# One layer of a hybrid decoder: residual sums of the last stage on PE, and square roots that take raw sums

## The chip, the cores and the metric

The kernel runs on one core of a Trainium2 chip. The metric is the device time of one execution in microseconds (us). All arithmetic is fp32 but for a few index tables. The engines are PE (matrix products), DVE (vector), ACT (scalar functions), POOL and SP, which here issues most DMAs. The kernel is written engine by engine: each engine runs its own list of instructions in the order written, and the lists meet at semaphores.

## The reference

The whole is one decoder layer on 1024 prompt tokens and 8 x 8 sample tokens, with a convolution group, an RWKV-7 group and a two-level mixture of experts. What matters for the change are the norms:

```python
def rmsnorm(x, g):
    xf = x.astype(jnp.float32)
    y = xf * lax.rsqrt(jnp.mean(xf * xf, axis=-1, keepdims=True) + RMS_EPS)
    return (y * g.astype(jnp.float32)).astype(x.dtype)
...
    xn = rmsnorm(x, norm1_g)
    proj = xn @ w_in
...
    var = jnp.mean(jnp.square(y - mu), axis=-1, keepdims=True)   # per head, in rwkv_mixer
    y_n = ((y - mu) * lax.rsqrt(var + GN_EPS)).reshape(B, T, C_RWKV)
...
    h = x + jnp.concatenate([conv_out, rwkv_out], axis=-1) @ w_out
    h = h + hier_moe(rmsnorm(h, norm2_g), ...)      # each token: the weighted sum of two experts
...
    y_prompt = rmsnorm(h_p, norm_f_g)
    y_sample = rmsnorm(h_s, norm_f_g)
```

D_MODEL is 1024, a head has 64 channels, TOP_K is 2.

## The kernel before

The 1088 tokens are cut into NT = 9 tiles: tiles 0 to 7 have 128 prompt tokens each, tile 8 has the 64 sample tokens. A tile has its tokens on the partitions and 1024 columns.

**Start.** For each tile SP loads the rows of x. ACT squares them with a running total (`square`, L980) and takes the root (`root`, L986); DVE forms mean plus epsilon between the two (`mean_square`, L2151), then the reciprocal and the scaled tile (`scale`, L2157). PE transposes the tile in eight pieces (L1465), and ACT and DVE copy one half of the transposes each (`copy_T`). DVE's loop (L2176 to L2182) is: the mean square of tile i+1, the scaling of tile i, the copy of tile i-1. From tile 5 on PE also does two of the eight steps of the first projection's first piece after each tile (L1472). When all tiles are through, PE transposes the small tables (L1447 to L1454) and goes on with the projection (L1616). The loads are issued in the order: tile 0, the gain, tiles 1 to 8 with two weight loads among them, 18 small tables, further weights.

**Middle.** The group norm of the RWKV part takes its variances with a reduction and then a multiply-add on DVE (`gn_variance`, L2436), a root on ACT (`gn_root`) and a reciprocal on DVE. The second norm has the same chain as the first (`square2` on ACT, `norm2` on DVE), tile by tile, while PE does the output projection.

**Experts.** The turns of the expert loop leave for each token two weighted-to-be rows in DRAM, `y_rows`, and PE, ACT and DVE finish the last group at about the same time.

**Tail.** SP reads the pairs of rows of the nine tiles in the order `LAST`, tile i into `yk[i]` (L734 to L736). `hres[i]`, in SBUF, is the residual of tile i; `w_k` holds the two weights of each token. For the tiles in `ON_PE`, ACT builds two diagonal matrices from the weights (`diag`), and PE forms the weighted sum of the pair in two PSUM banks, `rows_bank(i)`, as products with them: two halves of 512 columns, two rows each (L2134). There are four such pairs of banks, so the fifth and sixth tile wait until DVE has read the first and second (`ff_done`). Ahead of them PE does 72 products of the identity with itself, whose result nobody reads (L2125). On DVE `combine(i)` (L2846) adds the PSUM sum to the residual, or, for the other tiles, does two multiply-adds from `yk` (L2854). ACT squares the result with a running total (L1431), DVE forms mean plus epsilon (`last_mean_square`), ACT takes the root (L1437), and DVE takes the reciprocal and scales by the last gain into `fin[i]` (`last_scale`, L2868). SP stores each tile (L732). DVE's list is a pipeline over three tiles: combine n, mean square n-1, scale n-2.

```python
LAST = [0, NT - 1, 1, 2, 3, 4, *range(5, NT - 1)]
ON_PE = [1, 2, 3, 5, 6, 7]
```

Of the kernel before, what the change touches and what calls it, by code (L numbers as in the profile page):

```python
# [10 lines left out]
ALU = mybir.AluOpType  # L11
# [60 lines left out]
def hybrid_decoder_step(nc, x_prompt, x_sample, state_conv, state_shift, state_wkv, norm1_g, w_in, conv_w, conv_b,  # L72
# [5 lines left out]
    with ctx:  # L78
# [291 lines left out]
        sq_done, ms_done, std_done, xn_done = sem("sq_done"), sem("ms_done"), sem("std_done"), sem("xn_done")  # L370
# [120 lines left out]
        LAST = [0, NT - 1, 1, 2, 3, 4, *range(5, NT - 1)]  # L491
        ON_PE = [1, 2, 3, 5, 6, 7]
# [7 lines left out]
        ff_done, fin_done = sem("ff_done"), sem("fin_done")  # L500
        fin_out = [sem(f"fin_out{s}") for s in range(2)]
# [17 lines left out]
        def _(sp):  # L519
# [213 lines left out]

            for i in LAST:  # L734
                r = rows_of(i)
                sp.dma_start(yk[i][0:r, :, :], y_pairs[i * P:i * P + r, :, :]).then_inc(yk_in[i], 16)  # L736
# [242 lines left out]
        def _(act):  # L979
# [18 lines left out]
            act.wait_ge(iota_done, 1)  # L998
# [194 lines left out]
            def gn_root(i):  # L1193
                v = gvar[:, 0:4 * chunks_of(i)]
                act.wait_ge(gvar_done, i + 1)
                act.activation(v, v, ACT.Sqrt).then_inc(gstd_done, 1)
# [126 lines left out]
            def square2(i):  # L1323
                r = rows_of(i)
                act.wait_ge(h_done, i + 1)
                act.activation(squares2[0:r, :], hres[i][0:r, :], ACT.Square, accum_out=stat[0:r, 4, i:i + 1])\
                    .then_inc(sq_done, 1)
                act.wait_ge(ms_done, NT + i + 1)
                act.activation(stat[0:r, 6, i:i + 1], stat[0:r, 5, i:i + 1], ACT.Sqrt).then_inc(std_done, 1)
# [96 lines left out]
            for n in range(NT + 1):  # L1426
                if n < NT:
                    i = LAST[n]
                    r = rows_of(i)
                    act.wait_ge(ff_done, n + 1)  # L1430
                    act.activation(fin_sq[i][0:r, :], hres[i][0:r, :], ACT.Square, accum_out=stat[0:r, 0, i:i + 1])\  # L1431
                        .then_inc(sq_done, 1)
                if n >= 1:
                    i = LAST[n - 1]
                    r = rows_of(i)
                    act.wait_ge(ms_done, 2 * NT + n)
                    act.activation(stat[0:r, 2, i:i + 1], stat[0:r, 1, i:i + 1], ACT.Sqrt).then_inc(std_done, 1)  # L1437

        @block.tensor
        def _(pe):  # L1440
# [683 lines left out]
            for n in range(72):  # L2124
                pe.matmul(banks(7)[:, 0:P], ident[:, :], ident[:, :], start=True, stop=True)  # L2125
            for n, i in enumerate(ON_PE):
                b = rows_bank(i)
                pe.wait_ge(diag_ready, 2 + n)
                pe.wait_ge(yk_in[i], yk_0[i] + 16)
                if n >= 4:  # L2130
                    pe.wait_ge(ff_done, LAST.index(ON_PE[n - 4]) + 1)
                for half in range(2):
                    for k in range(TOPK):
                        ins = pe.matmul(banks(b + half), diag[:, k, i, :], yk[i][:, k, half * 512:half * 512 + 512],  # L2134
                                        start=(k == 0), stop=(k == TOPK - 1))
                ins.then_inc(rows_psum, 1)

        @block.vector
        def _(dve):
# [9 lines left out]
            dve.memset(stat[:, 7, 2:3], 0.5)  # L2149
            dve.memset(hx[:, :, 0:HB], 0.0)  # L2150
            def mean_square(i):  # L2151
                r = rows_of(i)
                dve.wait_ge(sq_done, i + 1)
                dve.tensor_scalar(stat[0:r, 1, i:i + 1], stat[0:r, 0, i:i + 1], 1.0 / D, RMS_EPS, ALU.mult, ALU.add)\
                    .then_inc(ms_done, 1)

# [279 lines left out]
            def gn_variance(i):  # L2436
                v = gvar[:, 0:4 * chunks_of(i)]
                dve.wait_ge(gsq_done, i + 1)
                dve.wait_ge(yn_done, i)
                link(dve.tensor_reduce(v, groups(gsq[i], i), AX.X, ALU.add))  # L2440
                dve.tensor_scalar(v, v, 1.0 / HD, GN_EPS, ALU.mult, ALU.add).then_inc(gvar_done, 1)
# [149 lines left out]
            def norm2(i):  # L2591
                r = rows_of(i)
                dve.wait_ge(sq_done, NT + i + 1)
                dve.tensor_scalar(stat[0:r, 5, i:i + 1], stat[0:r, 4, i:i + 1], 1.0 / D, RMS_EPS, ALU.mult, ALU.add)\
                    .then_inc(ms_done, 1)
# [250 lines left out]
            def combine(i):  # L2846
                r = rows_of(i)
                if i in ON_PE:
                    dve.wait_ge(rows_psum, NT + ON_PE.index(i) + 1)
                    dve.tensor_tensor(hres[i], banks(rows_bank(i), 2), hres[i], ALU.add).then_inc(ff_done, 1)  # L2850
                    return
# [9 lines left out]
            def last_mean_square(n):  # L2861
                i = LAST[n]
                r = rows_of(i)
                dve.wait_ge(sq_done, 2 * NT + n + 1)
                dve.tensor_scalar(stat[0:r, 1, i:i + 1], stat[0:r, 0, i:i + 1], 1.0 / D, RMS_EPS, ALU.mult, ALU.add)\
                    .then_inc(ms_done, 1)

            def last_scale(n):  # L2868
# [6 lines left out]
                dve.wait_ge(ff_done, n + 1)  # L2875
                dve.scalar_tensor_tensor(out=fin[i][0:r, :], in0=hres[i][0:r, :], scalar=stat[0:r, 3, i:i + 1],
                                         in1=gain_f[0:r, :], op0=ALU.mult, op1=ALU.mult).then_inc(fin_done, 1)

            for n in range(NT + 2):
                if n < NT:  # L2880
# [36 lines left out]
```

## Time and profile before

| | us |
|---|---|
| median of 3 runs | 1195.33 |
| the runs | 1194.43, 1199.28, 1195.33 |
| the profiled execution, its own time | 1193.24 |
| its span in the profile | 1191.5 |
| PE busy | 1125.2 (94% of the span) |
| DVE busy | 669.5 (56%) |
| ACT busy | 362.9 (30%) |
| mean granted clock of PE, as a share of full speed | 0.977 |

In the chain of work that ended last, the products of the input projection (L1616) have 27%, those of the expert loop (L2077, L2107) 15% and 8%, the output projection (L1927) 9%. Busy times of PE are modelled, so the start of a product is to be trusted more than its length. Times in the rows count from the start of the span.

### The profile page before, as it was taken

Reading aid. Unit: us, or ns where it says so; the run is one execution under the profiler, and the core shown is the slowest. Engines: PE = TensorE matmul, PEld = TensorE weight load, DVE = VectorE, ACT = ScalarE, POOL = GpSimd, SP = SyncE. Lnnn points to the kernel's source line nnn. Section 1 sums busy time; section 2 is a strip of 40 time slices with the busy share of each in tenths; the row PEclk is TensorE's granted clock in tenths of the full one; section 3 lists DMA queues with packets and bytes.
Section 4 is the critical chain, followed back from the end, with each engine's and each line's share of the span. In section 5 each row is a group of like instructions: output and inputs, shape, how many; then the busy total and the mean of one; then the engine's idle time right before and its main releaser. Section 6 shows DMA issues by size and latency. Waiting matters only on the chain.

```text
span 1191.5 us, 24463 instructions
## 1 busy us (share of the span) xinstructions
PE 1125.2 (94%) x9496; PEld 683.2 (57%) x9497; DVE 669.5 (56%) x1177; ACT 362.9 (30%) x722; POOL 221.0 (19%) x280
## 2 busy tenths in 40 slices
PE   5999999999998899999989999986999999999986
PEld 4666666666556688998985555544333333333362
DVE  5188999992224578888853332455434343434327
ACT  5100001111212556767742221122133232322232
POOL 5000000010002212333320011001223333333100
PEclk9999999999999899999999999987999999999999
DMA  9111111110000111111125322138899899999657
GB/s 288 51 36 36 36 37 38 41 42 22 1 1 5 16 16 17 16 20 19 19 48 189 106 62 71 45 138 337 340 372 323 306 331 342 415 411 407 267 180 311
DMA packets 97293, 171.44 MB, mean 144 GB/s; under 512 B 44377, under 2 KB 68624, under 8 KB 87921
## 3 DMA queue, kind: packets, MB, share of 16 engines
q1 hardware_dynamic: 89713, 152.31, 36.1%
q0 software_dynamic: 7488, 17.84, 4.3%
q8 instruction: 66, 1.08, 0.4%
q14 instruction: 26, 0.21, 0.1%
HBM read 153.63 MB, written 25.91 MB: 151 GB/s over the span
## 4 chain that ended last, share of the span: by engine, by line
PE 84%; DVE 9%; DMA 2%; ACT 2%; issue 2%; SPq 0%; DVEq 0%; ACTq 0%; POOLq 0%
PE ps L1616 27%; PE ps L2077 15%; PE ps L1927 9%; PE ps L2107 8%; PE ps L1628 6%; PE ps L1649 3%; PE ps L2064 2%; DVE arena L2390 1%; PE ps L1637 1%; PE ps L2125 1%; PE ps L1957 1%; DVE arena L2393 1%; PE ps L1515 1%; DMA arena<-in_w_exp_up_dram 1%; PE ps L2134 1%
## 5 line engine op out<-in xcount | busy, mean ns | idle before, releaser
L1616 PE MATMUL ps<-arena 128*128 128x384 f32 (+1 forms) x1040 | 318.9, 468 | 0.0
L1616 PEld LDWEIGHTS ps<-arena 128*128 128x128 f32 x1040 | 196.9, 190 | 118.6 <-issue 1.4
L2077 PE MATMUL ps<-arena 128*64 x416 | 188.5, 596 | 3.1 <-DVE arena L2791 2.2
L2080 PE MATMUL ps<-arena 128*64 128x512 f32 x416 | 188.5, 596 | 0.0
L2227 DVE SCALAR_TENSOR_TENSOR arena<-arena,cw 128x1024 f32<-128x1024 f32 x240 | 168.2, 778 | 0.4
L2077 PEld LDWEIGHTS ps<-arena 128*64 128x64 f32 x416 | 54.5, 136 | 111.3 <-issue 111.3
L1927 PE MATMUL ps<-arena 128*128 128x512 f32 x256 | 113.1, 596 | 0.0
L1628 PE MATMUL ps<-arena 64*64 64x64 f32 x2960 | 100.0, 219 | 6.6 <-DMA arena<-x_blocks 1.9
L1628 PEld LDWEIGHTS ps<-arena 64*64 64x64 f32 x2960 | 93.1, 135 | 10.0 <-issue 5.4
L2107 PE MATMUL ps<-arena 128*64 x208 | 96.5, 607 | 2.4 <-ACT arena L1395 2.4
L2110 PE MATMUL ps<-arena 128*64 128x512 f32 x208 | 96.5, 607 | 0.0
L1927 PEld LDWEIGHTS ps<-arena 128*128 128x128 f32 x256 | 47.5, 190 | 57.1 <-issue 57.0
L839 POOL COPY lastz<-arena 128x1 f32<-128x1 f32 x14 | 11.4, 813 | 328.8 <-ACT arena L1113 328.8
L1107 ACT ACTIVATE arena<-ps 128x768 f32<-128x768 f32 x14 | 11.4, 812 | 195.8 <-PE ps L1616 195.8
L933 POOL DMA_INDIRECT late<-xn_rows,g_idx x24 | 64.5, 2686 | 20.4 <-POOL g_idx L930 20.4
L2812 DVE COPY arena<-arena 128x4096 f32 x26 | 59.4, 2283 | 8.2 <-SPq L674 6.4
L2797 DVE TENSOR_TENSOR small<-ps,small 128x256 f32<-128x256 f32 x26 | 11.0, 425 | 89.7 <-ACT small L1379 89.7
L2280 DVE TENSOR_TENSOR arena<-arena 128x1024 f32<-128x1024 f32 x14 | 17.1, 1222 | 72.0 <-ACT arena L1113 72.0
L2107 PEld LDWEIGHTS ps<-arena 128*64 128x64 f32 x208 | 26.8, 138 | 53.0 <-issue 53.0
L2080 PEld LDWEIGHTS ps<-arena 128*64 128x64 f32 x416 | 54.5, 136 | 0.0
L2821 DVE COPY arena<-ps 128x256 f32<-128x256 f32 x26 | 11.0, 424 | 76.6 <-PE ps L2093 76.6
L1395 ACT ACTIVATE arena<-arena 128x2048 f32 x26 | 49.6, 1908 | 14.1 <-SPq L678 12.9
(357 smaller groups left out, 1552.4 us busy)
## 6 DMA issues: line engine op xcount, KB each, us to landing
arena<-in_w_exp_gate_dram SPq DMA_DIRECT2D x32, 1024.0 KB, 8.2
arena<-in_w_exp_up_dram SPq DMA_DIRECT2D x32, 1024.0 KB, 10.9
arena<-in_w_exp_down_dram SPq DMA_DIRECT2D x32, 1024.0 KB, 10.0
arena<-in_w_in_dram SPq DMA_DIRECT2D x22, 512.0 KB, 4.1
arena<-in_x_prompt_dram SPq DMA_DIRECT2D x16, 512.0 KB, 7.8
arena<-y_rows SPq DMA_DIRECT2D x8, 1024.0 KB, 15.1
arena<-in_w_out_dram SPq DMA_DIRECT2D x2, 2048.0 KB, 10.6
xn_rows<-arena SPq DMA_DIRECT2D x8, 512.0 KB, 2.9
```

The source lines that it names most:

```text
L933: pool.indirect_dma_start(out=xg[b], out_offset=None, in_=xn2_rows, in_offset=bass.IndirectOffsetOnAxis(ap=g_idx[b][:, :], axis=0), bounds ...
L1395: act.activation(wd.rearrange("p c n -> p (c n)"), wring[:, bass.ds(slot, 1), 2 * DC * F:].rearrange("p a n -> p (a n)"), ACT.Copy)\
L1616: ins = pe.matmul(banks(proj_bank(q) + piece)[:, 0:n1 - n0], win[q % 6][:, c, :], xnT[:, c, n0:n1], start=(c == 0), stop=(c == DC - 1))
L1628: ins = pe.matmul(dst[h, hp * 64:hp * 64 + 64], lhs[h, hp, :], rhs[h, hp, :], start=alone or (first and hp == 0), stop=alone or last, skip ...
L1649: ins = pe.matmul(banks(2 + c)[h, hp * P:(hp + 1) * P], lhs[h, hp, t], AR[j % 3][h, hp, :, t], start=True, stop=True)
L1927: ins = pe.matmul(banks(2 * (i % 2) + half)[0:r, :], lhs, wout[c // CT][:, c % CT, half * 512:half * 512 + 512], start=(c == 0), stop=(c = ...
L2077: pe.matmul(banks(b)[0:HS, :], xgT[b][:, c, 0:HS], wring_gu[:, bass.ds(slot, 1), 0:2, c, :].rearrange("p a w f -> p (a w) f"), start=(c == ...
L2080: ins = pe.matmul(banks(b)[HS:P, :], xgT[b][:, c, HS:P], wgu[b][:, :, c, :], start=(c == 0), stop=(c == DC - 1))
L2107: pe.matmul(banks(5 + half)[0:HS, :], hT[:, c, 0:HS], wring[:, bass.ds(slot, 1), n0:n0 + 512].rearrange("p a n -> p (a n)"), start=(c == 0 ...
L2110: ins = pe.matmul(banks(5 + half)[HS:P, :], hT[:, c, HS:P], wd[:, c, half * 512:half * 512 + 512], start=(c == 0), stop=(c == 1))
L2227: dve.scalar_tensor_tensor(out=dst, in0=src, scalar=w, in1=dst, op0=ALU.mult, op1=ALU.add).then_inc(conv_tap, 1)
L2812: dve.tensor_copy(wgu[b].rearrange("p w c f -> p (w c f)"), wring[:, bass.ds(slot, 1), 0:2 * DC * F].rearrange("p a n -> p (a n)"))\
```

## The change

There are four parts.

1. Two constants, RMS_EPS and GN_EPS, are written to `stat` once, and each root takes the raw sum, with 1/D or 1/HD as its scale and the constant as its bias. The mean squares on DVE are gone, in all three norms and in the group norm. ACT waits for its own square instead.
2. In the tail five tiles (1, 2, 3, 5, 6) are on PE, and tile 7 joins 0, 4 and 8 on DVE. PE also adds the residual, as a product with the identity that opens each sum in PSUM; for the first four tiles ahead of all row pairs. The unread products ahead are 48 instead of 72. The fifth tile waits for the scaling of the first (`fin_done`).
3. ACT's square and DVE's last scaling read the complete sum of such a tile straight from PSUM. `combine` is left for tiles 0, 8, 4 and 7 alone.
4. DVE's list in the tail is written out anew, and the order of tiles 6 and 7 is exchanged in the scalings and the stores. The rows are read in the same order as before (`READ`).

```diff
-        LAST = [0, NT - 1, 1, 2, 3, 4, *range(5, NT - 1)]
-        ON_PE = [1, 2, 3, 5, 6, 7]
+        LAST = [0, NT - 1, 1, 2, 3, 4, 5, 7, 6]
+        ON_PE = [1, 2, 3, 5, 6]
...
+        def summed(i):
+            return banks(rows_bank(i), 2) if i in ON_PE else hres[i][0:rows_of(i), :]
...
             def root(i):
                 r = rows_of(i)
-                act.wait_ge(ms_done, i + 1)
-                act.activation(stat[0:r, 2, i:i + 1], stat[0:r, 1, i:i + 1], ACT.Sqrt).then_inc(std_done, 1)
+                act.wait_ge(sq_done, i + 1)
+                act.activation(stat[0:r, 2, i:i + 1], stat[0:r, 0, i:i + 1], ACT.Sqrt, scale=1.0 / D,
+                               bias=rms_eps[0:r, :]).then_inc(std_done, 1)
...
-            for n in range(72):
+            for n in range(48):
                 pe.matmul(banks(7)[:, 0:P], ident[:, :], ident[:, :], start=True, stop=True)
+
+            def residual_in(i):
+                for half in range(2):
+                    pe.matmul(banks(rows_bank(i) + half), ident[:, :], hres[i][:, half * 512:half * 512 + 512],
+                              start=True, stop=False)
+
+            for i in ON_PE[0:4]:
+                residual_in(i)
             for n, i in enumerate(ON_PE):
                 b = rows_bank(i)
                 pe.wait_ge(diag_ready, 2 + n)
+                if n == 4:
+                    pe.wait_ge(fin_done, LAST.index(ON_PE[0]) + 1)
+                    residual_in(i)
                 pe.wait_ge(yk_in[i], yk_0[i] + 16)
-                if n >= 4:
-                    pe.wait_ge(ff_done, LAST.index(ON_PE[n - 4]) + 1)
...
-            mean_square(0)
             for i in range(NT):
-                if i + 1 < NT:
-                    mean_square(i + 1)
                 scale(i)
                 if i >= 1:
                     copy_T(i - 1)
...
-                dve.wait_ge(ff_done, n + 1)
-                dve.scalar_tensor_tensor(out=fin[i][0:r, :], in0=hres[i][0:r, :], scalar=stat[0:r, 3, i:i + 1],
+                dve.scalar_tensor_tensor(out=fin[i][0:r, :], in0=summed(i), scalar=stat[0:r, 3, i:i + 1],
                                          in1=gain_f[0:r, :], op0=ALU.mult, op1=ALU.mult).then_inc(fin_done, 1)
 
-            for n in range(NT + 2):
-                if n < NT:
-                    combine(LAST[n])
-                if 1 <= n <= NT:
-                    last_mean_square(n - 1)
-                if n >= 2:
-                    last_scale(n - 2)
+            combine(LAST[0])
+            combine(LAST[1])
+            for n in range(NT):
+                last_scale(n)
+                if n == 3:
+                    combine(4)
+                if n == 6:
+                    combine(7)
```

DVE's list at the start of the program, before. `arena<-arena,stat,gain` is the scaling, `arena<-ps` the copy of transposes:

```order
L2154 TENSOR_SCALAR stat<-stat 128x1 [waits sq_done] x2
L2160 RECIPROCAL stat<-stat 128x1 [waits std_done]
L2165 SCALAR_TENSOR_TENSOR arena<-arena,stat,gain 128x1024 [waits gain1_in,dve_chain]
L2154 TENSOR_SCALAR stat<-stat 128x1 [waits sq_done]
L2160 RECIPROCAL stat<-stat 128x1 [waits std_done]
L2165 SCALAR_TENSOR_TENSOR arena<-arena,stat,gain 128x1024 [waits dve_chain]
L2172 COPY arena<-ps 128x4x128 [waits xT_psum]
```

The same place in the changed kernel:

```order
L2174 RECIPROCAL stat<-stat 128x1 [waits std_done]
L2179 SCALAR_TENSOR_TENSOR arena<-arena,stat,gain 128x1024 [waits gain1_in,dve_chain]
L2174 RECIPROCAL stat<-stat 128x1 [waits std_done]
L2179 SCALAR_TENSOR_TENSOR arena<-arena,stat,gain 128x1024 [waits dve_chain]
L2186 COPY arena<-ps 128x4x128 [waits xT_psum]
```

The scaling of tile 0 no longer has an instruction ahead of it that waits for tile 1's square.

DVE's list in the tail, before, from tile 8's multiply-adds on to the scaling of tile 1 (`shift` is the buffer of `w_k`, `late` the last gain):

```order
L2854 SCALAR_TENSOR_TENSOR arena<-arena,shift 64x1024 [waits dve_chain]
L2865 TENSOR_SCALAR stat<-stat 128x1 [waits sq_done]
L2850 TENSOR_TENSOR arena<-ps,arena 128x1024 [waits gb_psum]
L2865 TENSOR_SCALAR stat<-stat 64x1 [waits sq_done]
L2872 RECIPROCAL stat<-stat 128x1 [waits std_done]
L2876 SCALAR_TENSOR_TENSOR arena<-arena,stat,late 128x1024 [waits ff_done,tables2_in,dve_chain]
L2850 TENSOR_TENSOR arena<-ps,arena 128x1024 [waits gb_psum]
L2865 TENSOR_SCALAR stat<-stat 128x1 [waits sq_done]
L2872 RECIPROCAL stat<-stat 64x1 [waits std_done]
L2876 SCALAR_TENSOR_TENSOR arena<-arena,stat,late 64x1024 [waits ff_done,dve_chain]
```

The changed kernel, from the scaling of tile 2 to that of tile 5:

```order
L2871 SCALAR_TENSOR_TENSOR arena<-ps,stat,late 128x1024 [waits dve_chain]
L2857 SCALAR_TENSOR_TENSOR arena<-arena,shift 128x1024 [waits w_loaded4]
L2857 SCALAR_TENSOR_TENSOR arena<-arena,shift 128x1024 [waits dve_chain]
L2868 RECIPROCAL stat<-stat 128x1 [waits std_done]
L2871 SCALAR_TENSOR_TENSOR arena<-ps,stat,late 128x1024 [waits dve_chain]
L2868 RECIPROCAL stat<-stat 128x1 [waits std_done]
L2871 SCALAR_TENSOR_TENSOR arena<-arena,stat,late 128x1024 [waits dve_chain]
L2868 RECIPROCAL stat<-stat 128x1 [waits std_done]
L2871 SCALAR_TENSOR_TENSOR arena<-ps,stat,late 128x1024 [waits dve_chain]
```

The additions and mean squares are out of the list, the scalings of tiles on PE read `ps`, and tile 4's multiply-adds stand between the scalings of tiles 2 and 3.

PE's list in the tail of the changed kernel (before, the 72 unread products were followed by six groups of four row-pair products and nothing else):

```order
L2134 MATMUL ps<-ident 128x128 x47
L2138 MATMUL ps<-arena,ident 128x512 x8
L2152 MATMUL ps<-arena 128x512 [waits w_loaded1,tanh_done]
L2152 MATMUL ps<-arena 128x512 x3
L2152 MATMUL ps<-arena 128x512 [waits w_loaded2,tanh_done]
L2152 MATMUL ps<-arena 128x512 x3
L2152 MATMUL ps<-arena 128x512 [waits w_loaded3,tanh_done]
...
L2138 MATMUL ps<-arena,ident 128x512 [waits fin_done,tanh_done]
L2138 MATMUL ps<-arena,ident 128x512
L2152 MATMUL ps<-arena 128x512 [waits x_loaded0]
```

Eight residual products (`arena,ident`) now stand between the unread products and tile 1's row pairs, and two more ahead of tile 6's.

## Rows read from the trace of the kernel before

**Rows 1.** The page's chain that ended last, shares of the span by engine.

```profile
PE 84%; DVE 9%; DMA 2%; ACT 2%; issue 2%; SPq 0%; DVEq 0%; ACTq 0%; POOLq 0%
```

**Rows 2.** Timeline of SP: start, length, engine, line, operation, out<-in, count.

```profile
1.26 0.42 SPq L530 DMA_DIRECT2D gain<-in_norm_g_dram  x1
...
8.90 4.89 SPq L522 DMA_DIRECT2D arena<-in_x_sample_dram  x1
...
21.56 7.79 SPq L526 DMA_DIRECT2D arena<-in_w_in_dram  x4
```

**Rows 3.** The same loads in the DMA view: count, KB, us from issue to landing.

```profile
gain<-in_norm_g_dram SPq DMA_DIRECT2D x1, 512.0 KB, 5.2
...
arena<-in_x_sample_dram SPq DMA_DIRECT2D x1, 256.0 KB, 12.6
...
arena<-in_w_in_dram SPq DMA_DIRECT2D x1, 512.0 KB, 8.1
```

**Rows 4.** Timeline of DVE at the start; in brackets the idle time before.

```profile
9.21 1.28 DVE L2165 SCALAR_TENSOR_TENSOR arena<-arena,stat,gain 128x1024 f32<-128x1024 f32 x1
...
21.81 0.15 DVE L2160 RECIPROCAL stat<-stat 128x1 f32<-128x1 f32 x1
...
23.20 0.69 DVE L2172 COPY arena<-ps 128x512 f32<-128x512 f32 x1
```

**Rows 5.** PE at the start: timeline, then stretches of L1465 (after the dash PEclk, DMA, GB/s).

```profile
23.34 1.97 PE L1465 MATMUL ps<-ident,arena 128*128 128x128 f32 x8 [0.95 <-DVE arena L2165]
...
33.54 0.26 PE L1447 MATMUL ps<-ident,arena 50*128 50x50 f32 x1
...
15.90:19.80 3.90, 3.77 (x16) 3.13 (x16) 1.00 1.08 255
21.30:22.40 1.10, 1.09 (x8) 0.85 (x8) 1.00 1.06 232
23.30:25.30 2.00, 1.96 (x8) 1.57 (x8) 0.50 1.04 225
```

**Rows 6.** Timeline of ACT at the start, the root of tile 1.

```profile
9.14 0.20 ACT L989 ACTIVATE stat<-stat 128x1 f32<-128x1 f32 x1 [0.22 <-DVE stat L2154]
```

**Rows 7.** Timeline of ACT near 518 us, without and with a bias from SBUF.

```profile
518.06 0.63 ACT L1024 ACTIVATE arena<-arena 128x512 f32<-128x512 f32 x1 [0.41 <-DVE arena L2235]
518.72 0.72 ACT L1026 ACTIVATE arena<-arena,stat 128x512 f32<-128x512 f32 x1
```

**Rows 8.** The chain in order of time, second norm of tile 8: start, length, what.

```profile
790.89 0.16 DVE stat L2594
```

**Rows 9.** Timeline of DVE in the tail.

```profile
1154.30 2.60 DVE L2854 SCALAR_TENSOR_TENSOR arena<-arena,shift 128x1024 f32<-128x1024 f32 x2 [9.90 <-DMA arena<-y_rows]
...
1164.33 1.22 DVE L2850 TENSOR_TENSOR arena<-ps,arena 128x1024 f32<-128x1024 f32 x1 [4.57 <-PE ps L2134]
...
1171.20 1.22 DVE L2850 TENSOR_TENSOR arena<-ps,arena 128x1024 f32<-128x1024 f32 x1 [0.77 <-PE ps L2134]
...
1187.16 1.29 DVE L2876 SCALAR_TENSOR_TENSOR arena<-arena,stat,late 128x1024 f32<-128x1024 f32 x1
```

**Rows 10.** Groups by line and shape, 1143 to 1192: count, busy us, mean ns, idle before.

```profile
L2850 DVE TENSOR_TENSOR arena<-ps,arena 128x1024 f32<-128x1024 f32 x6 | 7.3, 1221 | 6.1 <-PE ps L2134 6.1
...
L1431 ACT ACTIVATE arena<-arena 128x1024 f32<-128x1024 f32 x8 | 8.5, 1057 | 23.4 <-DVE arena L2850 13.0 <-DVE arena L2854 10.4
...
L1431 ACT ACTIVATION_READ_ACCUMULATOR arena<-arena 128x1 f32 x8 | 1.5, 187 | 0.0
```

**Rows 11.** Lines 2125 and 2134 on PE: ns min/median/max, first and last start.

```profile
L2125 PE MATMUL ps<-ident x144: 275/275/347, 1144.5 to 1160.6; 128*128 128x128 f32 x144
...
L2134 PE MATMUL ps<-arena x48: 592/592/595, 1160.7 to 1180.9; 128*128 128x512 f32 x48
```

**Rows 12.** Line 736, the nine reads of row pairs: ns each, first and last issue.

```profile
L736 SPq DMA_DIRECT2D arena<-y_rows x9: 344/469/655, 1148.6 to 1152.9; - x9
...
DMA to landing us min/median/max: 5.7/15.1/21.8
```

More of the change, by code:

```diff
@@ L490, in hybrid_decoder_step @@
         diag = at(O_ZS + NT * D, TOPK, NT, P)
-        LAST = [0, NT - 1, 1, 2, 3, 4, *range(5, NT - 1)]
-        ON_PE = [1, 2, 3, 5, 6, 7]
+        READ = [0, NT - 1, *range(1, NT - 1)]
+        LAST = [0, NT - 1, 1, 2, 3, 4, 5, 7, 6]
+        ON_PE = [1, 2, 3, 5, 6]
+        ON_DVE = [i for i in LAST if i not in ON_PE]
+        assert len(ON_PE) == 5 and len(LAST) == NT
         diag_ready, rows_psum = tanh_done, gb_psum
@@ L732, in result_out @@
                 sp.dma_start(dst, fin[i][0:r, :]).then_inc(fin_out[n % 2], 16)
-            for i in LAST:
+            for i in READ:
                 r = rows_of(i)
@@ L1195, in gn_root @@
                 act.wait_ge(gvar_done, i + 1)
-                act.activation(v, v, ACT.Sqrt).then_inc(gstd_done, 1)
+                act.activation(v, v, ACT.Sqrt, scale=1.0 / HD, bias=gn_eps).then_inc(gstd_done, 1)
             def gn_affine(i, b):
@@ L1327, in square2 @@
                     .then_inc(sq_done, 1)
-                act.wait_ge(ms_done, NT + i + 1)
-                act.activation(stat[0:r, 6, i:i + 1], stat[0:r, 5, i:i + 1], ACT.Sqrt).then_inc(std_done, 1)
+                act.wait_ge(sq_done, NT + i + 1)
+                act.activation(stat[0:r, 6, i:i + 1], stat[0:r, 4, i:i + 1], ACT.Sqrt, scale=1.0 / D,
+                               bias=rms_eps[0:r, :]).then_inc(std_done, 1)
             def copy_T2(i):
@@ L1425, in _ @@
             act.activation(stat[:, 7, 0:1], stat[:, 7, 1:2], ACT.Sqrt)
-            for n in range(NT + 1):
-                if n < NT:
[L1428 to L1437, printed above, removed]
+            for n in range(NT):
+                i = LAST[n]
+                r = rows_of(i)
+                if i in ON_PE:
+                    act.wait_ge(rows_psum, NT + ON_PE.index(i) + 1)
+                else:
+                    act.wait_ge(ff_done, ON_DVE.index(i) + 1)
+                act.activation(fin_sq[i][0:r, :], summed(i), ACT.Square, accum_out=stat[0:r, 0, i:i + 1])\
+                    .then_inc(sq_done, 1)
+                act.wait_ge(sq_done, 2 * NT + n + 1)
+                act.activation(stat[0:r, 2, i:i + 1], stat[0:r, 0, i:i + 1], ACT.Sqrt, scale=1.0 / D,
+                               bias=rms_eps[0:r, :]).then_inc(std_done, 1)
         @block.tensor
@@ L2134, in _ @@
                         ins = pe.matmul(banks(b + half), diag[:, k, i, :], yk[i][:, k, half * 512:half * 512 + 512],
-                                        start=(k == 0), stop=(k == TOPK - 1))
+                                        start=False, stop=(k == TOPK - 1))
                 ins.then_inc(rows_psum, 1)
@@ L2149, in _ @@
             dve.memset(stat[:, 7, 2:3], 0.5)
+            dve.memset(stat[:, 7, 4:5], RMS_EPS)
+            dve.memset(stat[:, 7, 5:6], GN_EPS).then_inc(eps_ready, 1)
             dve.memset(hx[:, :, 0:HB], 0.0)
[L2151 to L2155, printed above, removed]
             def scale(i):
@@ L2439, in gn_variance @@
                 dve.wait_ge(yn_done, i)
-                link(dve.tensor_reduce(v, groups(gsq[i], i), AX.X, ALU.add))
-                dve.tensor_scalar(v, v, 1.0 / HD, GN_EPS, ALU.mult, ALU.add).then_inc(gvar_done, 1)
+                dve.tensor_reduce(v, groups(gsq[i], i), AX.X, ALU.add).then_inc(gvar_done, 1)
             def gn_inverse(i):
@@ L2859, in combine @@
                 ins.then_inc(ff_done, 1)
[L2861 to L2866, printed above, removed]
             def last_scale(n):
@@ L2874, in last_scale @@
                     dve.wait_ge(tables2_in, 16 * 6)
[L2875 to L2876 removed]
+                dve.scalar_tensor_tensor(out=fin[i][0:r, :], in0=summed(i), scalar=stat[0:r, 3, i:i + 1],
                                          in1=gain_f[0:r, :], op0=ALU.mult, op1=ALU.mult).then_inc(fin_done, 1)
[L2879 to L2885 removed]
+            combine(LAST[0])
+            combine(LAST[1])
+            for n in range(NT):
+                last_scale(n)
[3 more added lines that the diff above has]
+                    combine(7)
 _INS = ['x_prompt', 'x_sample', 'state_conv', 'state_shift', 'state_wkv', 'norm1_g', 'w_in', 'conv_w', 'conv_b',
```

12 lines of the change are left out of this document (3 added, 9 removed).

## Prediction

> **What bounds the kernel now.** I read the page's chain first [rows 1]: PE carries 84% of it and DVE 9%, so an operation removed from DVE or ACT gains time only in the stretches where the chain leaves PE. I then went through the chain in order of time for each place that the diff touches. There are four: the start (tile norms ahead of the first projection), the group norm and the second norm (mostly beside PE's work), and the tail. In the start and in the tail DVE and ACT set the pace, and there I read each engine's own timeline.
>
> The profiled execution took 1193.24 us with a span of 1191.5. The shown runs have a median of 1195.33, so the sum below is made against 1193.24 and then carried over to the median. A difference of 0.5% is 6 us, about what a measurement of this kernel can tell from none.
>
> **Start: DVE's order loses a wait.** Before, DVE did the mean square of tile i+1 ahead of the scaling of tile i. Its scaling of tile 0 thus stood behind tile 1's square sum: it began at 9.21 us [rows 4], though tile 0's root had long been taken. With the mean squares gone, tile 0's scaling waits for its root and for the gain alone. The gain's load is issued at 1.26 and lands 5.2 us later [rows 2, 3], at about 6.5. That is 2.7 us earlier for the first transposes, and ACT, which copies tile 0's transposes before it squares tile 3, moves up as well.
>
> After that each tile needs on DVE a reciprocal, a scaling and a copy. From reciprocal to the end of the copy these take 21.81 to about 23.85 [rows 4], so 2.05 us. Before, the scalings of tiles 0 and 5 began at 9.21 and 22.0 (right behind the reciprocal at 21.81) [rows 4], 2.55 us a tile, because DVE's extra wait for the next tile's sum closed a ring DVE, PE, ACT, DVE over two tiles. Afterwards I place tile 1's scaling at 9.4 (its square waits for its data and its root ended at 9.34 [rows 6], now near 9.2) and then one tile in 2.05 us: tile 5's scaling starts at 9.4 + 4 x 2.05 = 17.6 and ends at 18.8. Before, PE began tile 5's transposes at 23.34 [rows 5], and from there it was busy up to 33.54, where the transposes of the tables begin: 10.2 us for four tiles and the interleaved eight-column pieces of the first projection. Same work from 18.8 ends at 29.0, that is 4.5 us earlier. PE goes on with the projection at once, and DVE, ACT and the later weight loads follow PE by their waits, so I see nothing that gives this back.
>
> Both ends of this term: the pace of PE's transposes differs by two within the start (16 passes in 3.8 us between 15.9 and 19.8, 8 in 1.1 us between 21.3 and 22.4, 8 in 2.0 us from 23.3 on; the clock is printed as 1.00 for the first two and 0.50 for the third [rows 5]). If PE is quick from tile 5 on, its four tiles need about 8.5 us, and the end is 27.3; but there the data stops it. Tile 8's rows land at 8.90 + 12.6 = 21.5, which still fits. The tables are issued before the weights that are issued at 21.56 and land 8.1 us later, at 29.7 [rows 2, 3]; that load is 0.5 MB, so the tables are there some 2 us sooner, near 27.9. This makes the largest gain 5.6 us. If the transposes of all four tiles run slowly, as 23.3 shows, they take 3 x 1.1 us more than in the quick case, and the end is about 30.5, a gain of 3. If the tables land just with the weights at 29.7, the gain is 3.8. I take 4.5, since rows 5 show one slow tile in this stretch and I leave it in.
>
> **The roots themselves.** ACT's root of a tile now takes the raw sum, with a bias read from SBUF, and waits for ACT's own square. Removed: ACT's idle time of 0.22 us ahead of a root [rows 6], less a few hundredths for the new wait. Added: the bias operand. No root with one is in the trace; the nearest pair is ACT's 0.722 us with such a bias against 0.630 without, same shape [rows 7], so 0.09. Net 0.1 us a tile for the better. In the start it is inside the 9.4 above. In the second norm and the group norm PE works on meanwhile. The chain meets such a step at tile 8 of the second norm, 0.16 us at 790.89 [rows 8], and once in the group norm, about as long. Sum for both, less the bias: **0.3 us**, with ends 0 and 0.5.
>
> **Tail: the DVE list.** Before, DVE's last stretch ran from the row pairs of tile 0 at 1154.30 to the end of the last scaling at 1188.45, and from 1171.20 on it hardly idled [rows 9]. Its work there: 3 tiles of two multiply-adds, 6 additions of PE's pair sum to the residual (1.22 us each [rows 10]), 9 mean squares, 9 reciprocals and 9 scalings. The change takes away the 6 additions and the mean squares (7.3 us and about 0.06 of its own time for each mean square, 0.5) and puts in one more tile of multiply-adds, 2.55 us: DVE loses 5.3 us of work. It doesn't get all of it, since now every scaling waits in turn for its square and root, with nothing of another tile between.
>
> PE first. The 144 passes of the 72 dummy products last from 1144.5 to 1160.6 [rows 11], 0.112 us each; 96 passes end at 1155.3. Then come the residuals of four tiles, two products of 512 columns a tile. A product is two passes in the trace (24 products of row pairs gave 48 passes between 1160.7 and 1180.9, 0.43 us each [rows 11]), so these are 16 passes, 6.9 us. The first pair sum thus starts at 1162.2, not at 1160.7; the rows are there, since the nine reads land 5.7 to 21.8 us after their issues from 1148.6 to 1152.9 [rows 12], the last one (tile 7) at 1174.7. With 8 passes a tile, 3.43 us, and 0.2 until DVE sees the sum (1164.33 in [rows 9] for 1160.7), the sums of tiles 1, 2, 3 and 5 are ready at 1165.8, 1169.2, 1172.6 and 1176.0, and tile 6, with its own residual (12 passes), at 1181.2. Its wait for the third scaling costs nothing: that is done near 1168.6.
>
> From a sum to its scaling: a square of 1.06 and a read of its total of 0.19, which overlap by 0.1 [rows 10]; a root of 0.20 [rows 6] and 0.09 for its bias, and DVE's reciprocal, 0.19 before the scaling can start. That is about 1.4 + 0.2; a scaling takes 1.2 in a row of them. Walking down DVE's list:
> - tile 2's scaling starts at 1170.85 and ends at 1172.1 (DVE idles ahead of it);
> - tile 4's multiply-adds end at 1174.6, tile 3's scaling at 1176.0;
> - tile 4's at 1177.5 (ACT just keeps up), tile 5's at 1179.0;
> - tile 7's multiply-adds end at 1181.5; DVE waits 1.5 us for its square and root, and scales it by 1184.4;
> - tile 6's, ready on PE at 1181.2, is squared after tile 7's and scaled by 1185.9.
>
> Against 1188.45 this is **2.5 us** earlier. The same walk with the old list gives 1188.4, so its durations fit. The stores behind it stay: 3 us from the last scaling to the end of the span, as before.
>
> What bounds this term: no scaling from PSUM is in the trace. DVE's addition from PSUM takes 1.22 us [rows 10] and a scaling from SBUF 1.29 [rows 9], so PSUM need cost nothing; with 0.13 more for each of them and 0.1 more for ACT's squares the walk ends at 1186.6 (gain 1.8), with 0.05 less each and a root as short as before at 1185.4 (gain 3.0). The Trainium skill (VectorE: DVE Perf Modes, the section on the TRN2 errata) gives DVE 58 cycles of fixed cost from SBUF and 120 from PSUM, at 0.96 GHz an estimate of 0.06 us more for each of the scalings from PSUM; by it the tail's gain would be 2.3 instead of 2.5. The rows on the 1024-wide operations speak against it here.
>
> **Sum.** 4.5 + 0.3 + 2.5 = 7.3 us. On the profiled execution that gives 1185.9, on the median of the shown runs 1188.0. Profiled and plain runs can fall either side, so I forecast 1187.5.
>
> **Rivals.**
> *Start holds, tail doesn't (chance 0.12).* If PE's sums come a few us late (they are on the path up to tile 2, and again if tile 6's sum passes 1182.8), DVE waits and the tail ends where it did. For it: before, DVE had idled 4.6 us for tile 1 [rows 9], and the residuals delay that sum by another 1.5. Against: DVE has 5.3 us less to do. Time: 1195.3 - 4.8 = 1190.5.
> *Tail holds, start doesn't (0.17).* The ring in the start is really held by the data, or the pace of transposes halves, or the tables land late. For it: DMA moves data all through the first 30 us, and the tables come last. Against: the landings above. Left are 0.3 + 2.5 and perhaps 0.5: 1192.
> *Slower (0.05).* PE's clock falls in the tail. The dummy products are what keeps PE busy while the rows travel; a third of them goes. At the low level, where a transpose took 0.25 us instead of 0.14 or less [rows 5], each pass of 512 columns would take twice 0.43, 0.86. The path to tile 2's sum has 32 of them: 13.7 us more, less the 7.3, so 6.4 above the median: 1201.7. It decides from 17 slow passes on. Against: PE goes from dummies to residuals to pair sums with no idle time from 1144.5 to 1181.
> *The change does nothing* would be that DVE's wait for the root replaces the wait for the sum everywhere; that is true of the second norm and is counted there.
>
> **How the numbers follow.** My forecast has the rest, 0.66. Its own range follows from the bounds: gains of 3.0 to 5.6, 0 to 0.5, 1.8 to 3.0, so 4.8 to 9.1 below 1193.2 or 1195.3: 1184 to 1190.5. Taking in the second rival up to 1192.5 leaves out some 0.15. Over 0.5% faster means below 1189.4: 0.52 of my 0.66 (7.3 is not far above 6, and three runs spread by a few us), 0.04 of the first rival, 0.01 of the second: 0.57. Slower: 0.05 and a noisy pair of medians, 0.06. The rest, 0.37, is the same.
>
> **What would show it.** In the start: tile 0's scaling near 6.5, DVE at one tile in 2.05 us, the table transposes near 29. If they start at 31 or later, that step is wrong. In the tail: dummies up to 1155.3 (counted from their start, 10.8 us), first pair sum 17.7 us after it; DVE idle ahead of tiles 1, 2 and 7's scalings only; last scaling 31.6 us after the first multiply-add, where it was 34.15. Roots of 0.28 us. In between: the same distance from the table transposes to the first row read, within 1 us; if that distance grows, the gain of the start was given back there.

## The result and the profile after

The changed kernel takes 1186.70 us (median of 12 runs, 1182.63 to 1191.58) against 1194.47 for the kernel before (12 runs of the same comparison, 1191.49 to 1199.28). The ratio is 0.9936 with a 95% interval of 0.9922 to 0.9951: faster by 7.6 us, give or take 1.7. The forecast was 1187.5, from a sum of 7.3 us.

The profiled execution took 1186.2 us with a span of 1184.5, 7.0 us less than before. The stages, by their first instructions in the two traces, in us:

| stretch | before | after | difference |
|---|---|---|---|
| start of the span to the transposes of the tables | 33.54 | 28.26 | -5.3 |
| from there to the first unread product | 1111.0 | 1111.6 | +0.6 |
| from there to the end of the last scaling | 43.90 | 41.54 | -2.4 |
| from there to the end of the span | 3.05 | 3.10 | 0.0 |

DVE's timeline at the start of the changed kernel (start, length, engine, line, operation, count, in brackets the idle time before and what ended it):

```profile
5.92 0.16 DVE L2174 RECIPROCAL stat<-stat 128x1 f32<-128x1 f32 x1 [4.69 <-ACT stat L996]
6.64 1.28 DVE L2179 SCALAR_TENSOR_TENSOR arena<-arena,stat,gain 128x1024 f32<-128x1024 f32 x1 [0.56 <-DMA gain<-in_norm_g_dram]
9.37 0.17 DVE L2174 RECIPROCAL stat<-stat 128x1 f32<-128x1 f32 x1 [1.44 <-ACT stat L996]
...
18.15 1.28 DVE L2179 SCALAR_TENSOR_TENSOR arena<-arena,stat,gain 128x1024 f32<-128x1024 f32 x1
```

Tile 0's scaling starts at 6.64 instead of 9.21 ([rows 4]), and what it waits for is now the gain's load. The last line is tile 5, which starts at 18.15 where it started at 22.00. PE in the same stretch, from tile 4 on:

```profile
17.50 1.09 PE L1474 MATMUL ps<-ident,arena 128*128 128x128 f32 x8 [1.31 <-DVE arena L2179]
19.49 1.09 PE L1474 MATMUL ps<-ident,arena 128*128 128x128 f32 x8 [0.90 <-DVE arena L2179]
20.42 1.46 PE L1481 MATMUL ps<-arena 128*128 128x384 f32 x4
...
28.26 0.26 PE L1456 MATMUL ps<-ident,arena 50*128 50x50 f32 x1
```

Tile 5's transposes start at 19.49 instead of 23.34 and take 1.09 us, not 1.97 ([rows 5]).

ACT's root of tile 1, which answers to [rows 6], follows the read of the total at once. It is longer, 0.29 us for 0.20, so it ends at 9.33, where it ended at 9.34:

```profile
8.82 0.19 ACT L990 ACTIVATION_READ_ACCUMULATOR arena<-arena 128x1 f32 x1
9.04 0.29 ACT L996 ACTIVATE stat<-stat 128x1 f32<-128x1 f32 x1
```

The tail on DVE, from the scaling of tile 1 on:

```profile
1162.82 1.28 DVE L2871 SCALAR_TENSOR_TENSOR arena<-ps,stat,late 128x1024 f32<-128x1024 f32 x1
1166.06 0.16 DVE L2868 RECIPROCAL stat<-stat 128x1 f32<-128x1 f32 x1 [1.95 <-ACT stat L1445]
1166.26 1.28 DVE L2871 SCALAR_TENSOR_TENSOR arena<-ps,stat,late 128x1024 f32<-128x1024 f32 x1
1167.46 2.59 DVE L2857 SCALAR_TENSOR_TENSOR arena<-arena,shift 128x1024 f32<-128x1024 f32 x2
...
1174.39 2.60 DVE L2857 SCALAR_TENSOR_TENSOR arena<-arena,shift 128x1024 f32<-128x1024 f32 x2
1178.53 0.16 DVE L2868 RECIPROCAL stat<-stat 128x1 f32<-128x1 f32 x1 [1.54 <-ACT stat L1445]
...
1180.12 1.28 DVE L2871 SCALAR_TENSOR_TENSOR arena<-ps,stat,late 128x1024 f32<-128x1024 f32 x1
```

DVE idles 1.95 us ahead of tile 2's reciprocal and 1.54 ahead of tile 7's, and ends at 1181.40. PE's list behind it, without a gap from the unread products to the last row pair:

```profile
1139.86 10.96 PE L2134 MATMUL ps<-ident 128*128 128x128 f32 x96 [0.88 <-DVE small L2836]
1150.65 7.03 PE L2138 MATMUL ps<-arena,ident 128*128 128x512 f32 x16
1157.52 13.90 PE L2152 MATMUL ps<-arena 128*128 128x512 f32 x32
1171.25 1.88 PE L2138 MATMUL ps<-arena,ident 128*128 128x512 f32 x4
```

The operations on PSUM, in groups by line and shape (count, busy us, mean ns, idle before), DVE's scalings and then ACT's squares:

```profile
L2871 DVE SCALAR_TENSOR_TENSOR arena<-ps,stat,late 128x1024 f32<-128x1024 f32 x5 | 6.4, 1284 | 0.2
L2871 DVE SCALAR_TENSOR_TENSOR arena<-arena,stat,late 128x1024 f32<-128x1024 f32 x3 | 3.9, 1285 | 0.1
...
L1442 ACT ACTIVATE arena<-ps 128x1024 f32<-128x1024 f32 x5 | 5.1, 1017 | 8.9 <-PE ps L2152 8.9
L1442 ACT ACTIVATE arena<-arena 128x1024 f32<-128x1024 f32 x3 | 3.2, 1057 | 13.0 <-DVE arena L2857 13.0
```

### The profile page after: what moved, and what is told of

Read it like the earlier page. It is cut to its first block, busy times and chain, and to the rows that moved or that the text cites. A ratio compares the mean times of both kernels' runs of the same rounds, so it can differ in the third digit from the quotient of the medians.

```text
span 1184.5 us, 24342 instructions
## 1 busy us (share of the span) xinstructions
PE 1123.2 (95%) x9460; PEld 679.1 (57%) x9461; DVE 658.5 (56%) x1139; ACT 366.4 (31%) x720; POOL 223.9 (19%) x280
## 3 DMA queue, kind: packets, MB, share of 16 engines
q1 hardware_dynamic: 89713, 152.31, 36.2%
## 4 chain that ended last, share of the span: by engine, by line
PE 82%; DVE 10%; DMA 4%; ACT 2%; issue 2%; SPq 1%; DVEq 0%; ACTq 0%; POOLq 0%
PE ps L1625 27%; PE ps L2086 13%; PE ps L1936 9%; PE ps L2116 7%; PE ps L1637 6%; DMA arena<-in_w_exp_up_dram 3%; PE ps L1658 3%; PE ps L2073 2%; DVE arena L2401 1%; PE ps L1646 1%; PE ps L1966 1%; PE ps L2134 1%; DVE arena L2404 1%; PE ps L1524 1%; DVE arena L2367 1%
## 6 DMA issues: line engine op xcount, KB each, us to landing
arena<-in_w_out_dram SPq DMA_DIRECT2D x2, 2048.0 KB, 10.5
```

## The experiments

Theory: the start gains because DVE's wait for tile i+1's sum no longer stands ahead of tile i's scaling; the tail gains because DVE has less to do, with PE on the path up to tile 2's sum; the middle neither gains nor loses. The rivals: the gain of the start comes from the removed operations and their handovers; a later stage gives it back; the tail is bound by one engine alone.

Eight kernels were run, 4 to 12 times each: four on one chip beside 31 runs of the kernel before, and four on another beside 14. Below, "tables" is the first transpose of the tables, and "tail" is the time from the first unread product on PE to the start of the last scaling on DVE; each is read from the run's profile.

| kernel | ratio to before (95%) | tile 0's scaling | tables | tail |
|---|---|---|---|---|
| before | 1 | 9.2 | 33.5 | 42.6 |
| changed | 0.9936 (0.9922 to 0.9951) | 6.6 | 28.3 | 40.3 |
| start alone | 0.9943 (0.9921 to 0.9965) | 6.7 | 28.5 | 42.7 |
| mean squares kept, moved | 0.9979 (0.9958 to 0.9999) | 6.6 | 30.3 | 42.6 |
| changed, one wait put back | 0.9965 (0.9949 to 0.9981) | 9.3 | 34.2 | 40.3 |
| tail alone | 0.9970 (0.9953 to 0.9986) | 9.3 | 34.2 | 40.3 |
| changed, DVE's list reordered | 0.9914 (0.9896 to 0.9932) | 6.6 | 28.2 | 38.4 |
| the same with 40 unread products | 0.9872 (0.9851 to 0.9893) | 6.7 | 29.1 | 36.6 |
| changed, 72 unread products | 0.9964 (0.9946 to 0.9982) | 6.7 | 28.3 | 45.6 |
| reordered with 24 | 0.9898 (0.9874 to 0.9921) | 6.6 | 28.3 | 36.2 |

The ratio isn't the quotient of the two medians. These alone give 5.8 us less for the start alone, 3.0 with the wait put back and 13.8 for the one with 40, each inside the interval of its ratio but nearer to zero than the ratio says.

**The start alone.** The kernel before with the first norm's part of the change:

```diff
-                act.wait_ge(ms_done, i + 1)
-                act.activation(stat[0:r, 2, i:i + 1], stat[0:r, 1, i:i + 1], ACT.Sqrt).then_inc(std_done, 1)
+                act.wait_ge(sq_done, i + 1)
+                act.activation(stat[0:r, 2, i:i + 1], stat[0:r, 0, i:i + 1], ACT.Sqrt, scale=1.0 / D,
+                               bias=rms_eps[0:r, :]).then_inc(std_done, 1)
...
-            mean_square(0)
             for i in range(NT):
-                if i + 1 < NT:
-                    mean_square(i + 1)
                 scale(i)
```

> The kernel before, with the mean squares taken off DVE in the first norm alone (ACT's root takes the raw sum with a bias there). Theory: the gain of the start stands alone and PE keeps it; table transposes begin at 28.3 us (33.5 before), the whole is 5.3 us shorter, give or take 1.5 for stretches of low PE clock that fall elsewhere. Rival (the later stages give part of it back): table transposes at 28.3, but the whole under 3 us shorter.

Measured: tables at 28.5, and 0.9943, 6.8 us less (4.2 to 9.4). The gain of the start stands alone, and the plain runs keep it whole. The profiled execution alone would not have shown this: its span is 1188.2, only 3.3 less than before, since its middle took 1.7 us more (below). The transposes of the tables waited here for a load that they need, so the last of those loads landed near 28.5 in this run, and a shorter list on DVE can hardly bring the start below that:

```profile
28.54 0.26 PE L1450 MATMUL ps<-ident,arena 50*128 50x50 f32 x1 [0.22 <-DMA late<-in_w_gate_up_dram]
```

**The mean squares kept, but moved.** The kernel before with this edit alone; every operation is still done, and the root still waits for DVE:

```diff
-            mean_square(0)
             for i in range(NT):
-                if i + 1 < NT:
-                    mean_square(i + 1)
+                mean_square(i)
                 scale(i)
```

> The kernel before, with every mean square still on DVE, but in the first norm the one of tile i directly ahead of the scaling of tile i instead of the one of tile i+1. Theory (the place in DVE's list costs, not the operation): scaling of tile 0 near 6.6 us, tiles 2.3 us apart, table transposes near 30.3, about 3.3 us earlier than before. Rival (the operation and its handover through DVE cost): scaling of tile 0 early too, but the table transposes stay at 32.5 or later.

Measured: tile 0's scaling at 6.60, tiles from 1 on 2.4 to 2.7 us apart, tables at 30.3. DVE's timeline, the scalings of tiles 0, 1, 2 and 5:

```profile
6.60 1.28 DVE L2165 SCALAR_TENSOR_TENSOR arena<-arena,stat,gain 128x1024 f32<-128x1024 f32 x1 [0.64 <-DMA gain<-in_norm_g_dram]
...
9.61 1.28 DVE L2165 SCALAR_TENSOR_TENSOR arena<-arena,stat,gain 128x1024 f32<-128x1024 f32 x1
...
12.02 1.32 DVE L2165 SCALAR_TENSOR_TENSOR arena<-arena,stat,gain 128x1024 f32<-128x1024 f32 x1
...
19.38 0.17 DVE L2160 RECIPROCAL stat<-stat 128x1 f32<-128x1 f32 x1 [0.27 <-ACT stat L989]
19.58 1.29 DVE L2165 SCALAR_TENSOR_TENSOR arena<-arena,stat,gain 128x1024 f32<-128x1024 f32 x1
```

So 3.2 of the 5.3 us come with no operation removed, by its place in DVE's list. Of the remaining 2.0, 1.4 are there when tile 5's scaling starts (19.58 for 18.15). In this kernel the sum goes ACT, DVE, ACT, DVE for each tile, and DVE idles 0.27 us ahead of each reciprocal for ACT's root. The other 0.6 lie behind it, where PE's transposes of tile 5 took 1.70 us and not 1.09.

**One wait put back.** The changed kernel with a wait and no operation:

```diff
             for i in range(NT):
+                if i + 1 < NT:
+                    dve.wait_ge(sq_done, i + 2)
                 scale(i)
```

> The changed kernel, with one wait put back and no operation: ahead of the scaling of tile i in the first norm, DVE waits for the square sum of tile i+1. Theory (the wait closes the ring): scaling of tile 0 at 9.1 us again, table transposes at 33, the whole about 5 us longer than the changed kernel, so 2 to 3 us shorter than before. Rival (mean squares and handovers cost): tile 0 late, but the table transposes by 30.5, since tiles then follow at 2.05 us.

Measured: tile 0's scaling at 9.29, tables at 34.20. PE's timeline at tile 5 (the first line) and the tables:

```profile
23.49 1.97 PE L1474 MATMUL ps<-ident,arena 128*128 128x128 f32 x8 [0.88 <-DVE arena L2179]
...
34.20 0.26 PE L1456 MATMUL ps<-ident,arena 50*128 50x50 f32 x1
```

That is where the kernel with the tail alone has them (34.2), whose start is that of the kernel before. With the wait in place, taking nine mean squares off DVE is worth nothing that shows here. I had expected 33; the profiles of two kernels with the same start as before lie 0.7 us apart (33.5 and 34.2), which covers a part of the miss of 1.2. The whole is 4.2 us shorter than before (2.3 to 6.1), where 2 to 3 were expected; that is inside the interval.

**The tail alone.** The changed kernel with the first norm, the group norm and the second norm as before (the edit of the first norm is the reverse of the one above; nothing in the tail differs from the changed kernel). For the second norm:

```diff
-                act.wait_ge(sq_done, NT + i + 1)
-                act.activation(stat[0:r, 6, i:i + 1], stat[0:r, 4, i:i + 1], ACT.Sqrt, scale=1.0 / D,
-                               bias=rms_eps[0:r, :]).then_inc(std_done, 1)
+                act.wait_ge(ms_done, NT + i + 1)
+                act.activation(stat[0:r, 6, i:i + 1], stat[0:r, 5, i:i + 1], ACT.Sqrt).then_inc(std_done, 1)
...
+                dve.wait_ge(sq_done, NT + i + 1)
+                dve.tensor_scalar(stat[0:r, 5, i:i + 1], stat[0:r, 4, i:i + 1], 1.0 / D, RMS_EPS, ALU.mult, ALU.add)\
+                    .then_inc(ms_done, 1)
```

> The kernel before, with the change made in the tail alone; first norm, group norm and second norm as before. Theory: from the first unread product on PE to the end of the last scaling 41.5 us instead of 43.9, the whole 2.4 us shorter, give or take 1.5. Rival (the tail's gain needs the earlier parts, or comes from noise): below 1 us.

Measured: tail 40.3 instead of 42.6, and 3.6 us less in all (1.7 to 5.6). The stages agree with the table of the first section: 5 to 5.3 us from the start, 2.4 from the tail. The 6.8 us of the start alone and the 3.6 here add up to 10.4, more than the 7.6 of the whole change, but the three intervals are wide enough for that. The change to the group norm and the second norm was not run by itself.

**DVE's list reordered.** The changed kernel with the two multiply-add pairs one scaling earlier:

```diff
-                if n == 3:
+                if n == 2:
                     combine(4)
-                if n == 6:
+                if n == 5:
                     combine(7)
```

> The changed kernel, with tile 4's multiply-adds one scaling earlier on DVE (behind tile 1's scaling) and tile 7's one earlier (behind tile 4's). Theory (the tail's end hangs on DVE, which idles 2 us ahead of tile 2's reciprocal and 1.5 ahead of tile 7's): 1.8 us shorter; from the first unread product to the start of the last scaling 38.4 us instead of 40.2, and DVE idles under 0.5 us ahead of tile 7's reciprocal. Rival (PE's sums set the end): tile 6's sum is no earlier, under 0.5 us gained.

Measured: tail 38.4. DVE's timeline:

```profile
1159.65 2.59 DVE L2857 SCALAR_TENSOR_TENSOR arena<-arena,shift 128x1024 f32<-128x1024 f32 x2
1162.16 0.16 DVE L2868 RECIPROCAL stat<-stat 128x1 f32<-128x1 f32 x1
...
1172.05 0.16 DVE L2868 RECIPROCAL stat<-stat 128x1 f32<-128x1 f32 x1 [0.15 <-ACT stat L1445]
```

Tile 4's multiply-adds now fill the time ahead of tile 2's reciprocal, and DVE waits 0.15 us for tile 7's root, not 1.54. So in the changed kernel the end of the tail hung on the order of DVE's list, not on PE's last sum, which comes no earlier here (36.7 us after the first unread product in both). Now it does hang on it: ACT waits 0.21 us for PE's sum of tile 6 before its last square. What is left of DVE's idle time is 1.48 us ahead of tile 3's reciprocal and the wait for tile 1's sum.

**The same with 40 unread products.** The added edit:

```diff
-            for n in range(48):
+            for n in range(40):
```

> As the run before, with 40 unread products instead of 48. Theory (PE is on the path through the sums of tiles 1 and 2, and the rows of tile 1 have landed by then): all sums 1.8 us earlier, and the tail 36.6 us. Rival (the rows land later than thought, or DVE is the only bound): 38 us or more.

Measured: tail 36.6, and a ratio of 0.9872, the lowest of all, though the interval overlaps that of the run with 24. By the plain runs that is 15.3 us less than before (12.8 to 17.8); by the stages it is 4.5 from the start and 6.0 from the tail, so 10.5 (the two spans differ by 10.8). The difference of 5 us isn't accounted for by stages; part of it can be the scatter of the middle, and 1.5 of it goes if the medians are compared.

**72 unread products.** The changed kernel with:

```diff
-            for n in range(48):
+            for n in range(72):
```

> The changed kernel with the 72 unread products of before instead of 48. Theory (PE on the path up to tile 2's sum): every sum 5.4 us later, the tail 45.6 us instead of 40.2, so 3 us longer than that of the kernel before. Rival (DVE alone sets the end): the tail grows by under 2 us.

Measured: tail 45.6, 5.4 us more than with 48. That is 48 passes by 0.112 us, all of it on the path. PE's timeline and DVE's wait for tile 1:

```profile
1141.94 16.32 PE L2134 MATMUL ps<-ident 128*128 128x128 f32 x144 [0.89 <-DVE small L2836]
1158.10 7.03 PE L2138 MATMUL ps<-arena,ident 128*128 128x512 f32 x16
...
1170.07 0.16 DVE L2868 RECIPROCAL stat<-stat 128x1 f32<-128x1 f32 x1 [10.79 <-ACT stat L1445]
```

With the residuals on PE and the unread products as many as before, the tail is thus 3 us longer than that of the kernel before (45.6 for 42.6). The cut from 72 to 48 is not a trimming beside the change but what makes the tail's part pay. The opposite test, the kernel before with fewer unread products, was not run, and it is a rival for the tail. In that kernel DVE idled 4.57 us for tile 1's sum [rows 9]. Its first row pair could start some 1.7 us earlier before it met the landing of tile 1's rows (14.5 us after the first unread product in the last run below, where it started at 16.15). So an estimated 1.7 of the tail's 2.4 us might have come from fewer unread products alone; the 6.0 us of the reordered list with 40 are beyond that estimate.

**24 unread products, reordered.** The kernel with the reordered list and:

```diff
-            for n in range(48):
+            for n in range(24):
```

> As the run with 40, with 24 unread products. PE then has residual products up to 1150 us or so and idles about 5 us until tile 1's rows land. If PE keeps its clock over that idle time: tail 36.6 us, as with 40, since the rows set the start. If the clock falls to the low level in it: passes of 512 columns take 0.86 us for some us, and the tail is 39 us or more.

Measured: tail 36.2. PE idled 2.0 us for tile 1's rows, and its passes kept their length, at a granted clock of 1.00 throughout. DVE waited for rows too, the last of them tile 7's:

```profile
1142.63 7.03 PE L2138 MATMUL ps<-arena,ident 128*128 128x512 f32 x16
1151.67 13.97 PE L2152 MATMUL ps<-arena 128*128 128x512 f32 x32 [2.01 <-DMA arena<-y_rows]
```

```profile
1167.63 2.61 DVE L2857 SCALAR_TENSOR_TENSOR arena<-arena,shift 128x1024 f32<-128x1024 f32 x2 [1.03 <-DMA arena<-y_rows]
```

The idle time was 2.0 us and not the 5 I had written (the residual products alone last 6.9), so this doesn't show what a longer one does. It does show that fewer unread products help only until the rows bound the tail: tile 1's land near 1151.7 - 1137.2 = 14.5 us after the first one, and tile 7's near 30.4. The last scaling starts 0.5 us earlier than with 40, but what follows it up to the end of the span takes 3.85 us and not 3.21, so from the first unread product to the end it is 41.3 us against 41.1. Going from 40 to 24 gains nothing.

## Why the prediction was right

**The start.** Both halves of the argument hold: the scaling of tile 0 waits for the gain (6.64, predicted 6.5), tile 1's starts at 9.57 (9.4), and tile 5's at 18.15 (17.6). The moved mean squares and the wait put back show that the cause is the wait in DVE's order. The term came out as 5.3 us where 4.5 was taken, inside its 3.0 to 5.6, from two errors of opposite sign. Tile 5's transposes began at 19.49 and not at 18.8, since tile 4's scaling took 1.73 us instead of 1.28 and tile 1's root ended no earlier than before. From there to the tables PE took 8.8 us and not 10.2: I had left one slow tile in that stretch, as [rows 5] had it, and its pace was mis-sized. In the changed kernel the transposes ran slowly for tiles 0 to 2 alone and quickly from 15.05 on. (The interleaved work that I called eight-column pieces is products of 384 columns.) The tables' landing, which I had put near 27.9, didn't hold PE at 28.26, so it was no later than that; with the start alone it held PE until 28.54. My upper bound of 5.6 was thus nearly reached.

**Nothing gives it back.** Shown in the plain runs by the start alone (6.8 us less, 4.2 to 9.4) and, less directly, by the changed kernel.

**The middle.** Predicted 0.3 us less, measured 0.6 more in the pair of profiles. The local step did shrink: at tile 8 of the second norm ACT gets from its square to the end of the root in 1.47 us, where it took 1.63:

```profile
784.72 1.06 ACT L1334 ACTIVATE arena<-arena 64x1024 f32<-64x1024 f32 x1 [7.76 <-DVE arena L2597]
785.68 0.19 ACT L1334 ACTIVATION_READ_ACCUMULATOR arena<-arena 64x1 f32 x1
785.90 0.29 ACT L1337 ACTIVATE stat<-stat 64x1 f32<-64x1 f32 x1
```

But the middle as a whole scatters far more than that: from the tables to the first unread product the profiles show 1109.2 to 1112.7 us for the four kernels with the middle of before, and 1107.3 to 1113.6 for the six with the changed one. In one stretch the cause is plain. From the last product of line 1589 of the kernel before to the first of line 1927, the six kernels with the changed middle (changed, 72, wait put back, 40, reordered, 24) took 79.2, 79.2, 77.9, 77.2, 76.6 and 76.5 us. The first two have a granted clock below 1 in two places of it, the next two in one, the last two in none. The changed kernel, two stretches of 4 us (busy us and instructions of PE, PEld, DVE, ACT, POOL, then PEclk, DMA share, GB/s):

```profile
592.00:596.00 4.00, 4.00 (x92) 4.00 (x89) 3.58 (x8) 0.77 (x2) 0.95 (x1) 0.57 0.71 159
620.00:624.00 4.00, 4.00 (x100) 4.00 (x99) 2.28 (x5) 3.22 (x7) 0.00 (x0) 0.66 0.97 334
```

and the reordered one:

```profile
592.00:596.00 4.00, 4.00 (x130) 4.00 (x128) 2.28 (x4) 3.02 (x10) 1.04 (x1) 1.00 0.63 140
620.00:624.00 4.00, 2.74 (x94) 2.60 (x90) 1.84 (x3) 0.97 (x3) 1.04 (x1) 1.00 1.02 414
```

PE is busy throughout in both at 592, with 92 matrix instructions in 4 us at the low clock and 130 at the full one. The 0.3 us were never measurable in the whole.

**Luck in the sum.** The three terms came to 7.0 us against 7.3 because their errors cancel: the start gave 0.8 more than taken, the middle 0.9 less, which is scatter, and the tail 0.1 less. The terms of the start and the tail are borne out by themselves; the closeness of the sum is not a merit of theirs.

**The tail.** Step by step against the first unread product at 1139.86: predicted first residual 10.8 us after it, measured 10.79; tile 1's sum 21.25, ACT starts on it at 21.29; tile 2's scaling 26.3, measured 26.40; end of tile 7's multiply-adds 36.95, measured 37.1; end of the last scaling 41.35, measured 41.54. The term was 2.4 for 2.5. That PE is on the path up to tile 2's sum is shown by the run with 72. The reordered list shows that the two idle times of DVE which the walk found were the ones that counted. What the walk doesn't say is how much of the 2.4 us the smaller number of unread products would have brought by itself (see the run with 72).

**PSUM as a source.** DVE's scaling takes 1.284 us from PSUM and 1.285 from SBUF, and ACT's square 1.017 from PSUM and 1.057 from SBUF. By the Trainium skill's table (VectorE: DVE Perf Modes, the section on the TRN2 errata) the scaling should have been about 0.06 us longer from PSUM, an estimate. The trace shows no difference; for ACT the table's 52 cycles less from PSUM, at its 1.2 GHz an estimate of 0.043 us, agree with the 0.040 measured.

**The rivals.** None came about. The slower one, a fall of PE's clock in the tail, has nothing for it: the passes keep their 0.43 us even with a third of the original unread products and an idle time of 2 us. From what stretch of idleness they would slow down was not tried.

## What to carry to other kernels

In an in-order engine, look at what a cheap operation waits for, not at what it costs: a 0.15 us operation for the next tile, put ahead of the work on this one, tied DVE, PE and ACT into a ring by its wait, and cost 5 us in nine tiles. Moving it alone brought three of them, and removing it with the wait left in place brought none. When work is added to an engine that is kept busy with products that nobody reads, take as many of them off, and count both against the arrival of the data. Test too what taking them off brings by itself; that is missing here. In a list in which every step waits for the one before, put independent work into the longest of those waits.

## What I had not expected of the hardware

Ten kernels with nearly the same middle differ there by up to 6 us (1107.3 to 1113.6) in their profiled executions. Each has stretches of low granted clock in it. Cut into windows of 4 us, and with each window's length times the part of the clock that it lacks added up, the middle lacks 18.8 us in the two shortest (1107.3 and 1108.9), 20.5 to 23.9 in the seven between, and 25.6 in the longest. Some of these stretches, like the two above, fall where PE is fully busy. In the part between the lines 1589 and 1927 one such stretch went with 0.6 to 1.4 us more, and two with 2.6 to 2.7. What places them is open: four kernels with the same code up to the tail and the tables within 0.15 us (changed, reordered, 72 and 24) have two stretches in that part, none, two and none. So the profile of a single execution can't tell a gain of 1 or 2 us anywhere but in its own stage.

In the start, too, the pace of the same transposes changes at a different tile from kernel to kernel: the eight of tile 5 took 1.97 us before and with the wait put back, 1.70 with the mean squares moved, and 1.09 in the changed kernel. The granted clock printed there doesn't always follow the pace. It was 0.50 for the 1.97 us of tile 5, but 1.00 for the changed kernel's tile 0, which took 1.94 (first line), as for its tile 5 (second line; line 1474 alone: busy us and instructions of PE and PEld, then PEclk, DMA share, GB/s):

```profile
8.00:10.10 2.10, 1.94 (x8) 1.57 (x8) 1.00 1.04 391
19.40:20.60 1.20, 1.09 (x8) 0.86 (x8) 1.00 0.96 121
```
